# The transposes of h in the two FFN loops: 32 by 32 blocks on VectorE in place of eight TensorE transposes a step

## The reference

```python
def swiglu(h, w_gate, w_up, w_down):
    return (jax.nn.silu(h @ w_gate) * (h @ w_up)) @ w_down

x = x + 0.5 * swiglu(rms_norm(x, norm_ffn1_w[l]), ffn1_w_gate[l], ffn1_w_up[l], ffn1_w_down[l])
x = x + head_group_mixer(rms_norm(x, norm_mix_w[l]), w_in[l], attn_sinks[l], ret_gn_w[l], w_out[l])
x = x + 0.5 * swiglu(rms_norm(x, norm_ffn2_w[l]), ffn2_w_gate[l], ffn2_w_up[l], ffn2_w_down[l])
return rms_norm(x, norm_final_w)
```

## Time and profile before

| what | value |
|---|---|
| median of 3 runs | 1844.33 us (1844.28 to 1844.54) |
| the profiled execution | 1844.38 us |
| its span, first to last instruction | 1842.6 us |
| granted TensorE clock, of full speed | 0.999 |
| PE busy, matmuls | 1830.3 us, 99% |
| DVE busy | 1045.0 us, 57% |
| ACT busy | 832.0 us, 45% |
| POOL busy | 63.3 us, 3% |
| DMA | 346.61 MB, 188 GB/s |

### The profile page before, as it was taken

The page is one execution under the profiler, slowest core; times in us unless marked ns, Lnnn a source line. Parts: engine busy times, 40 slices in busy tenths (PEclk is TensorE's granted clock), DMA queues, the critical chain, the costliest instruction groups (busy, mean ns, idle before and its releaser), DMA issues.

```text
span 1842.6 us, 23062 instructions
## 1 busy us (share of the span) xinstructions
PE 1830.3 (99%) x8570; PEld 1537.5 (83%) x8570; DVE 1045.0 (57%) x1087; ACT 832.0 (45%) x996; POOL 63.3 (3%) x59
## 2 busy tenths in 40 slices
PE   9999999999999999999999999999999999999998
PEld 7888888888888888999998888888888888888886
DVE  5565465455556557555557665555555556546546
ACT  7444443444444444555555455444444444444344
POOL 0000000000000000000009000000000000000000
PEclk9999999999999999999999999999999999999999
DMA  9565555555555555555555456555556565565552
GB/s 367 195 194 186 193 190 186 197 185 191 195 183 187 200 183 172 179 179 167 172 160 180 137 182 206 183 190 197 183 192 193 184 195 190 187 195 188 190 198 92
DMA packets 177345, 346.61 MB, mean 188 GB/s; under 512 B 6048, under 2 KB 31008, under 8 KB 177184
## 3 DMA queue, kind: packets, MB, share of 16 engines
q1 hardware_dynamic: 176880, 345.61, 57.0%
q10 hardware_dynamic: 432, 0.55, 0.1%
HBM read 344.04 MB, written 2.10 MB: 188 GB/s over the span
## 4 chain that ended last, share of the span: by engine, by line
PE 98%; DMA 0%; DVE 0%; issue 0%; ACT 0%; SPq 0%; POOLq 0%; POOL 0%; DVEq 0%
PE ps L325 32%; PE ps L327 32%; PE ps L326 32%; PE ps L352 2%; DMA raw<-in_g 0%; PE ps L477 0%; PE ps L561 0%; PE ps L572 0%; PE ps L490 0%; PE ps L446 0%; PE ps L445 0%; PE ps L444 0%; DVE x L895 0%; DVE proj L1082 0%; DVE w_lo L846 0%
## 5 line engine op out<-in xcount | busy, mean ns | idle before, releaser
L846 DVE TENSOR_TENSOR w_lo<-raw,w_hi 128x1024 fp32r<-128x1024 f32 x656 | 812.9, 1241 | 770.6 <-ACT w_hi L636 770.0
L636 ACT ACTIVATE w_hi<-raw 128x1024 fp32r<-128x1024 f32 x656 | 695.0, 1061 | 979.9 <-PE ps L327 969.7
L325 PE MATMUL ps<-w_hi,xT_hi 128*128 128x512 f32 (+1 forms) x1848 | 714.6, 387 | 0.9 <-DVE xT_lo L859 0.9
L327 PE MATMUL ps<-w_hi,xT_lo 128*128 128x512 f32 (+1 forms) x1848 | 710.1, 384 | 0.0
L326 PE MATMUL ps<-w_lo,xT_hi 128*128 128x512 f32 (+1 forms) x1848 | 709.9, 384 | 0.0
L325 PEld LDWEIGHTS ps<-w_hi,xT_hi 128*128 128x128 f32 x1848 | 347.1, 188 | 63.7 <-DVE xT_lo L859 1.3
L327 PEld LDWEIGHTS ps<-w_hi,xT_lo 128*128 128x128 f32 x1848 | 347.0, 188 | 63.0
L326 PEld LDWEIGHTS ps<-w_lo,xT_hi 128*128 128x128 f32 x1848 | 347.2, 188 | 61.6
L325 PE MATMUL ps<-w_hi,hT_hi 128*128 128x512 f32 x640 | 249.1, 389 | 0.0
L327 PE MATMUL ps<-w_hi,hT_lo 128*128 128x512 f32 x640 | 249.0, 389 | 0.0
L326 PE MATMUL ps<-w_lo,hT_hi 128*128 128x512 f32 x640 | 249.0, 389 | 0.0
(11 more groups left out here) (109 smaller groups left out, 514.0 us busy)
## 6 DMA issues: line engine op xcount, KB each, us to landing
raw<-in_u SPq DMA_DIRECT2D x88, 1024.0 KB, 5.1
raw<-in_d SPq DMA_DIRECT2D x88, 1024.0 KB, 4.9
raw<-in_g SPq DMA_DIRECT2D x87, 1024.0 KB, 5.1
raw<-in_w_in SPq DMA_DIRECT2D x48, 896.0 KB, 4.6
raw<-in_w_out SPq DMA_DIRECT2D x16, 1024.0 KB, 4.9
x<-in_x SPq DMA_DIRECT2D x4, 512.0 KB, 12.7
out<-proj SPq DMA_DIRECT2D x8, 256.0 KB, 2.4
proj<-in_xT SPq DMA_DIRECT2D x3, 512.0 KB, 9.8
```

The source lines that it names most:

```text
L325: pe.matmul(out, xh, wh, start=first and j == 0, stop=False)
L327: mm = pe.matmul(out, xl, wh, start=False, stop=last and j == 1)
L636: act.activation(dst, raw[:, s, (k % 2) * HALF:(k % 2 + 1) * HALF], ACT.Copy).then_inc(hi_ready, 1)
L846: dve.tensor_tensor(w_lo[:, k % LEAD, :, :].rearrange(flat), raw[:, k // 2, (k % 2) * HALF:(k % 2 + 1) * HALF], f32(w_hi[:, k % LEAD, :, : ...
```

## The change

PE no longer turns h in the steps: turn_h and its waits for h_ready and x_added leave wide, and only the last block of each FFN is still turned by PE (turn_last_h, into banks 0 and 1). DVE's new turn_h does it instead, in eight parts of two instructions, one part behind the w_lo of each of the positions 0 to 7. An instruction reads 32 partitions of h (quarter src) with 2 tiles x 4 blocks x 32 columns, turns each 32x32 block, and writes it to the 32 partitions of quarter dst of banks 4 and 5. Sixteen of them, for each pair of src and dst, make up what eight transposes of 128x128 made. Part 0 waits for h_ready and x_added; the last instruction adds 2 to hT_turned. On ACT and on DVE hT goes from position 1 to position 9.

```diff
+SQ = 32
+TURNED = 8
...
-            def wide(norm, g, bank, h_of=None):
+            def wide(norm, g, bank):
...
-                    if h_of is not None and k == 1:
-                        turn_h(*h_of)
-
-            def turn_h(f, i, bank=B_DOWN):
-                c = NF * f + i
-                pe.wait_ge(h_ready, 2 * c + 2)
-                if bank == B_DOWN:
-                    pe.wait_ge(x_added, 4 * i + (X_FFN[f] - 1))
+
+            def turn_last_h(f):
+                pe.wait_ge(h_ready, 2 * (NF * f + NF - 1) + 2)
                 for b in range(2):
                     for j in range(2):
                         for t in range(T):
-                            mm = turn(bank + b, j * SEQ + t * P, h[:, t, (2 * b + j) * P:(2 * b + j + 1) * P])
+                            mm = turn(B_GATE + b, j * SEQ + t * P, h[:, t, (2 * b + j) * P:(2 * b + j + 1) * P])
                     mm.then_inc(hT_turned, 1)
...
-                        turn_h(f, NF - 1, B_GATE)
+                        turn_last_h(f)
...
-                    wide(None, g, B_GATE, h_of=(f, i - 1))
+                    wide(None, g, B_GATE)
...
                         position(g, k)
-                        if k == 1:
-                            hT(f, i - 1)
                         if k == 7:
                             silu(f, g, i)
+                        if k == TURNED + 1:
+                            hT(f, i - 1)
...
+            def turn_h(f, i, part):
+
+                if part == 0:
+                    dve.wait_ge(h_ready, 2 * i + (T * NF * f + 2))
+                    dve.wait_ge(x_added, 4 * i + (X_FFN[f] - 1))
+                for src in (2 * (part % 2), 2 * (part % 2) + 1):
+                    dst = part // 2
+                    out = ps[dst * SQ:(dst + 1) * SQ, B_DOWN:B_DOWN + 2, :].rearrange(
+                        "p b (j t c) -> p t (b j) c", j=2, t=T)[:, :, :, src * SQ:(src + 1) * SQ]
+                    blocks = h[src * SQ:(src + 1) * SQ, :, :].rearrange(
+                        "p t (k c) -> p t k c", k=4)[:, :, :, dst * SQ:(dst + 1) * SQ]
+                    m = dve.transpose(out, blocks)
+                if part == TURNED - 1:
+                    m.then_inc(hT_turned, 2)
+
...
-                        if k == 1:
+                        if k < TURNED:
+                            turn_h(f, i - 1, k)
+                        if k == TURNED + 1:
                             hT(f, i - 1)
```

## The result

| | before | after |
|---|---|---|
| median, 4 runs each | 1844.43 us | 1826.78 us (1826.59 to 1826.94) |
| ratio | | 0.9904, 95% interval 0.9892 to 0.9917 |
| span of the profiled execution | 1842.6 us | 1824.8 us |
| PE busy | 1830.3 us, x8570 | 1813.1 us, x8410 |
| DVE busy | 1045.0 us, 57% | 1190.8 us, 65% |

The account below looks back on a forecast made before the run. PE, busy 99% of the span, was taken to bound the kernel. Twenty groups of eight transposes at 0.88 us give 17.7 us, subtracted from 1844.33: 1826.6 us; range 1825.9 to 1830.0, the forecast's own 1826.2 to 1827.2.

Parts of the forecast that it names:

- PE's share: FFN steps on PE: removing eight transposes saves 0.88 us of its stream, 20 times, 17.7 us in all.
- The transposes on DVE: Sixteen added DVE instructions a step, positions 0 to 7: 0.45 us from one to the next, ends 0.27 and 1.23.
- The room: DVE per position: 2.72 us less 1.14 for w_lo leaves 1.58; two transposes take 0.90 and fit, up to 0.79 each.
- The lead of 5.57 us: Time w_lo at position 0 runs ahead of PE's half 4; PE waits only if slips over eight positions exceed it.
- What is moved: hT from position 1 to 9 on ACT and DVE: ACT doesn't wait, 3.2 us to spare; hT_lo 12 us; no cost.
- The slower case: Rival: DVE transposes too slow, PE waits for w_lo in halves 8 to 12; 11.8 us slower, 1856.1 us; chance 0.06.
- T: Time from one DVE transpose of h to the next in positions 0 to 7, taken as 0.45 us.
- The slowed stream: Rival: PE's matmuls beside DVE's PSUM-writing transposes lose 8 ns each, 5.1 us in all, 1831.7 us; chance 0.06.
- The rule on transposes: Skill's advice to use TensorE for full transposes, VectorE turning 32 by 32 blocks only; the prediction held it not decisive here.

Follow-up runs that it names:

- burst: The changed kernel with all sixteen DVE transposes of a step in one go behind position 0 and none behind 1 to 7; 1840.87 us.
- the run with five: The changed kernel with five DVE transposes instead of two behind each of positions 0 to 7, the fifth into unused SBUF; 1855.23 us.

## Why the prediction was right, point by point

- **PE's share.** 0.88 us for eight transposes, from the distance of two starts: the step went from 66.18 to 65.28 us (0.89 between the traces), the span to 1824.8 (1824.9 said), the median to 1826.78 (1826.6 said). The prediction's 17.7 is 20 times the unrounded 0.884; 20 x 0.88 is 17.6. The bar of 1.03 us for the eight would have given 20.6 us; the 160 mean bars of 272 ns would have given 43.5.
- **The transposes on DVE.** 0.45 us was taken between the rows of 256 elements; the bar is 0.456, the distance in a row 0.47. Neither end of the range (0.27, 1.23) came near. It was a choice between two rows of other operations, and the answer didn't hang on it: with four transposes a position, as if each of the two took twice as long, the time was the same.
- **The room.** 1.14 us for a w_lo was 0.11 too little where a transpose follows it (1.25), because I took the overlap from an add, whose operands start in the same quarter as w_lo's. DVE's rest per position is 0.45 to 0.62 us; I had said about 0.6.
- **The lead of 5.57 us.** Not needed by the change itself; with it used up (burst) PE's lateness is explained within 0.02 us a step.
- **What is moved.** ACT's hT_hi in position 9 doesn't wait; said 3.2 us to spare, measured 3.1. With four transposes a position ACT does wait there, 0.74 us, and the time stays.
- **The rivals.** The slower case is real but far: it begins between four and five transposes behind each w_lo, where the change has two. I had set it at T = 1.14 to 1.19 for two. With 1.25 us in place of 1.14 for the w_lo, and 0.12 us for a restart above the wait itself, the same sums give about 1.08 and 1.13 (an estimate; no run has two slow transposes a position). The slowed stream didn't show: 1826.89 without any DVE transpose.
- **The rule on transposes.** The prediction gives many small instructions as the reason of the rule that it cites. That is my reading; the section (the Trainium skill, "VectorE: DVE Perf Modes", The three transpose paths) says only that the 32 by 32 blocks are turned each by itself and don't make a full transpose. Here sixteen instructions a step made a full one of them, for 7.3 us of DVE's time and none of the kernel's.

## What to carry to other kernels

When one engine has no idle time, the worth of taking an instruction from it is the distance that it puts between its neighbours' starts; read it there, at the second neighbour behind if the first starts early, and check it on the period of the loop. The engine that takes the work over is judged by its lead over the bound engine: the new work may fill more than the gap of one position, as long as what it accumulates before the next quiet stretch stays under the lead. Where the moved work feeds the bound engine directly, as the last block's h does, that work has no lead, and what must be done from the last input to the first use has to fit by itself.

## What I had not expected of the hardware

- A restart of PE after a wait costs more than the idle bracket in the trace: 0.40 us in the bracket was 0.68 us of lateness (0.16 that the bar of the matmul before hides, 0.12 behind the restart).
- A wait of 2.1 us in PE's stream, in a kernel that had kept PE busy nearly without a break for 700 us, was followed, 1.0 us after the restart, by 3.2 us at half the clock in one of two places and by none in the other. With six transposes PE is up to 1.2 us late at a restart (0.83 to 1.02 in the brackets shown), four times a step, and the granted clock of that run is 0.999.
- The matmul behind a group of transposes starts 0.03 us after the last of them and passes 0.09 us of lateness on to its own follower: 0.79 us from the first transpose to the next matmul, but 0.88 us of the stream. The transposes themselves are 0.11 us apart all through.
- Two DVE instructions in a row overlap (by 0.06 to 0.09 us here) only where their inputs, and the last outputs to the same memory, start in the same quarter of the partitions.
- On DVE, 32 partitions x 256 elements take 0.456 us to transpose into PSUM, close to the 0.42 to 0.48 us of other instructions of 256 elements; into SBUF they took 0.436 (the run with five).
